# One kernel, one change: the RWKV-7 recurrence of a two-block transformer, from loops over pairs of heads to steps that work on three pairs at once, with 32-column inverses

## The chip, the cores and the metric

The kernel runs on one core of one Trainium2 chip. The metric is the time of one execution on the device in microseconds, as the median of several runs. PE is TensorE, DVE is VectorE, ACT is ScalarE, POOL is GpSimd, SP is SyncE.

## The reference, cut to what matters

The program is a whole network: two blocks with attention, gated linear attention and feed-forward parts over 512 tokens. The change touches one part of the second block, the recurrence of RWKV-7, with 8 heads of 64 features:

```
def rwkv7_scan(r, w, k, v, a_vec, b_vec):
    # per head, state S (N_v x N_k):
    # S_t = S_{t-1} diag(w_t) + (S_{t-1} a_t) b_t^T + v_t k_t^T ;  y_t = S_t r_t
    def step(state, inp):
        rt, wt, kt, vt, at, bt = inp
        sa = jnp.einsum('bhvk,bhk->bhv', state, at)
        state = state * wt[:, :, None, :] + sa[..., None] * bt[:, :, None, :] + vt[..., None] * kt[:, :, None, :]
        return state, jnp.einsum('bhvk,bhk->bhv', state, rt)
...
    kk = heads(k * rw_k_k, RW_N)
    kk = kk * lax.rsqrt(jnp.maximum(jnp.sum(kk * kk, -1, keepdims=True), 1e-24))
    k = k * (1 + (a - 1) * rw_k_a)
    y = rwkv7_scan(r_h, heads(decay, RW_N), k_h, v_h, -kk, kk * a_h)
...
    bonus = jnp.sum(r_h * k_h * rw_r_k, -1, keepdims=True) * v_h
```

The kernels compute it by chunks of 32 tokens. Inside of a chunk the recurrence is solved with the inverse of a triangular 32x32 matrix I - M, as the product of (I + M)(I + M^2)(I + M^4)(I + M^8)(I + M^16); across chunks a state is carried.

## The kernel before, in words

All is float32. Features lie on the 128 partitions (a pair of heads, 64 each), the 512 tokens along the free axis, as four tiles of 128 tokens, each of four chunks. `recurrence` (L3247) runs three stages one after another: `rwkv_prepare_stage` (decay, rate and gate), `rwkv_chunks_stage` (L2300 to L2733), which the change rewrites, and `rwkv_states_stage` (L2736), which carries the state over 16 chunks. No weights are loaded in this part.

`rwkv_chunks_stage` goes over four pairs of heads: a loop of three iterations on every engine and the last one as straight code (`over_pairs`, L2371). Every engine has its own order of work, and semaphores count its results. For a pair it does this:

- Operands, made one pair ahead by DVE, ACT and POOL between their other work: kk0, t, kx, scan, cx (`decays`, L2557), Ew, En, Ex (`exponentials`, L2671), the norm of the keys as a sum over a head by PE (`norm_sums`, L2453, one matmul of 512 columns), `reciprocal` of the whole 128x512 on DVE (L2577) and a square root on ACT (L2680), then kk, ah, bb, bh, kh, rk, rh and the bonus.
- PE (`pair`, L2460): TA, TB, TK and TV turn operands to tokens on partitions; BA, M and KA are products over the 64 features of each head, on the two halves of PE's rows (`fill_both`, L2423); DVE masks them to the chunk (L2620, L2627). A fill is what is written to one of seven PSUM banks, which are used in turn: a fill waits until the one seven places before has been taken by DVE or ACT (`free`, L2412).
- The inverse: M2, T2 (the square of M and of its transpose T), then for the powers 2, 4 and 8 a new M, a new T and X (the product so far), then X16. Each is a fill by `over_tiles` (L2434): four matmuls 128x128 by 128 columns, one per tile of tokens, of matrices that are zero outside of the four 32x32 blocks on the diagonal. ACT copies the new M and T (L2691), DVE adds X (L2636).
- P applies the inverse, Q are the queries, G the transitions and F the additions of the state of each chunk, Y the outputs inside of a chunk. For the sums over one chunk out of a tile's four, POOL writes copies of tok_b and tok_k with zeros in the other chunks' rows (Bm, Km, L2388), so that PE sums over all 128 rows: G as four matmuls of 256 columns per head (L2513), F as 64 matmuls of 64 columns (L2524, L2526).

POOL also multiplies the queries and G by decays (L2399, L2404) and copies v. At the start of the whole program POOL makes masks in a chain of single steps (`make_masks`, L139), ahead of the bias tables of the first attention (L1699 to L1717) and a DMA of the forget gates (L1678).

## Time and profile before

| | us |
|---|---|
| median of 3 runs | 2397.62 (2396.93 to 2399.07) |
| the profiled execution, its own time | 2404.41 |
| its span, first to last instruction | 2402.7 |
| busy in the span: PE, weight loads of PE (PEld), DVE, ACT, POOL | 2297.6, 1882.6, 1037.7, 870.6, 259.1 |
| PE instructions (records of matmuls) | 13903 |
| `rwkv_chunks_stage` in the span | 1036.0 to 1225.2 |
| mean granted clock of TensorE | 0.979 |

A busy PE is not PE at its peak, since matmuls overlap: a record's duration holds its passage through the array too. A float32 matmul leaves two records, and with each of them a weight load. What the engines do at one place is read from windows and timelines of that stretch, not from the shares of the span. The two slices of the page (60 us each) in which the DMA engines move almost nothing are those of this stage.

### The profile page before, as it was taken

What the parts mean: (1) busy time and instruction counts of PE and PEld (TensorE: products, weight loads), DVE (VectorE), ACT (ScalarE), POOL (GpSimd) and SP (SyncE); (2) the same over time, 40 slices, a digit from 0 to 9 for tenths busy, and PEclk for the clock granted to TensorE, in tenths of its full rate; (3) what the DMA queues carried; (4) which work ended last, traced back from release to release, by engine and by line L of the source; (5) the groups of instructions that cost most, each with busy time, mean ns of one, the idle gap of its engine ahead of it and who ended that gap; (6) DMA issues with size and microseconds to landing.
All of it is one profiled execution on the core that took longest, in us unless ns stands there. A gap on an engine that the chain in (4) does not pass through costs nothing. (4 is left out here: it accounts for less than half of the span.)

```text
span 2402.7 us, 33906 instructions
## 1 busy us (share of the span) xinstructions
PE 2297.6 (96%) x13903; PEld 1882.6 (78%) x13903; DVE 1037.7 (43%) x1593; ACT 870.6 (36%) x1511; POOL 259.1 (11%) x335
## 2 busy tenths in 40 slices
PE   8999999999999999879989999999999989999997
PEld 7777677988887877658868888888877779888886
DVE  4343335544334454356655443333533255333333
ACT  5444452423223352243413322222455544222223
POOL 4000000100000102023402200001422104000001
PEclk9999999999999999979999999999999999999998
DMA  5322123233333232100004233333242022333320
GB/s 163 84 53 61 46 80 88 77 99 96 95 92 93 63 105 71 37 0 1 0 2 114 74 99 96 97 92 93 71 86 60 19 77 73 94 99 98 96 87 36
DMA packets 346474, 178.38 MB, mean 74 GB/s; under 512 B 43927, under 2 KB 340037, under 8 KB 346333
## 3 DMA queue, kind: packets, MB, share of 16 engines
q1 hardware_dynamic: 344300, 171.54, 25.4%
q0 software_dynamic: 2032, 4.85, 0.7%
q8 instruction: 103, 1.69, 0.3%
q14 instruction: 39, 0.31, 0.0%
HBM read 171.35 MB, written 2.11 MB: 72 GB/s over the span
## 5 line engine op out<-in xcount | busy, mean ns | idle before, releaser
L428 DVE TENSOR_TENSOR w_lo<-w,w_hi 128x1024 fp32r<-128x1024 f32 (+2 forms) x327 | 398.1, 1220 | 437.9 <-ACT w_hi L421 437.5
L445 PE MATMUL bank<-act_hi,w_hi 128*128 128x512 f32 (+1 forms) x1496 | 564.9, 378 | 19.0 <-DVE act_lo L780 7.9
L447 PE MATMUL bank<-act_hi,w_lo 128*128 128x512 f32 (+1 forms) x1496 | 551.4, 369 | 0.0
L446 PE MATMUL bank<-act_lo,w_hi 128*128 128x512 f32 (+1 forms) x1496 | 550.1, 368 | 0.0
L421 ACT ACTIVATE w_hi<-w 128x1024 fp32r<-128x1024 f32 (+2 forms) x328 | 336.3, 1028 | 379.7 <-PE bank L447 255.9
L445 PEld LDWEIGHTS bank<-act_hi,w_hi 128*128 128x128 f32 x1496 | 284.0, 190 | 76.7 <-issue 15.0
L447 PEld LDWEIGHTS bank<-act_hi,w_lo 128*128 128x128 f32 x1496 | 283.9, 190 | 50.3
L446 PEld LDWEIGHTS bank<-act_lo,w_hi 128*128 128x128 f32 x1496 | 284.8, 190 | 46.2
L445 PE MATMUL bank<-hid_hi,w_hi 128*128 128x512 f32 (+1 forms) x560 | 207.7, 371 | 0.0
L447 PE MATMUL bank<-hid_hi,w_lo 128*128 128x512 f32 (+1 forms) x560 | 207.0, 370 | 0.0
L446 PE MATMUL bank<-hid_lo,w_hi 128*128 128x512 f32 (+1 forms) x560 | 206.4, 369 | 0.0
L445 PE MATMUL acc<-act_hi,w_hi 128*128 128x512 f32 (+1 forms) x480 | 175.6, 366 | 7.1 <-DVE act_lo L780 4.1
L446 PE MATMUL acc<-act_lo,w_hi 128*128 128x512 f32 (+1 forms) x480 | 174.3, 363 | 0.0
L447 PE MATMUL acc<-act_hi,w_lo 128*128 128x512 f32 (+1 forms) x480 | 174.2, 363 | 0.0
L663 DVE SCALAR_TENSOR_TENSOR x<-x,bank 128x512 f32<-128x512 f32 (+1 forms) x88 | 51.7, 588 | 192.5 <-PE bank L447 192.5
L445 PEld LDWEIGHTS bank<-hid_hi,w_hi 128*128 128x128 f32 x560 | 105.1, 188 | 21.0 <-issue 0.8
L446 PEld LDWEIGHTS bank<-hid_lo,w_hi 128*128 128x128 f32 x560 | 105.2, 188 | 20.2
L447 PEld LDWEIGHTS bank<-hid_hi,w_lo 128*128 128x128 f32 x560 | 105.3, 188 | 19.4
L445 PEld LDWEIGHTS acc<-act_hi,w_hi 128*128 128x128 f32 x480 | 91.7, 191 | 21.8 <-DVE w_lo L428 4.3
L447 PEld LDWEIGHTS acc<-act_hi,w_lo 128*128 128x128 f32 x480 | 91.6, 191 | 14.0
L446 PEld LDWEIGHTS acc<-act_lo,w_hi 128*128 128x128 f32 x480 | 91.7, 191 | 13.8
L714 ACT ACTIVATE hid_hi<-tmp_y 128x512 fp32r<-128x512 f32 (+1 forms) x48 | 28.6, 596 | 197.4 <-DVE tmp_y L724 197.4
(451 smaller groups left out, 3118.6 us busy)
## 6 DMA issues: line engine op xcount, KB each, us to landing
w<-in_ffn_w_gate_up SPq DMA_DIRECT2D x88, 512.0 KB, 3.8
w<-in_w_in SPq DMA_DIRECT2D x41, 512.0 KB, 3.9
w<-in_w_up SPq DMA_DIRECT2D x32, 512.0 KB, 4.0
w<-in_w_down SPq DMA_DIRECT2D x32, 512.0 KB, 3.9
w<-in_ffn_w_down SPq DMA_DIRECT2D x32, 512.0 KB, 4.0
w<-in_even_w_in SPq DMA_DIRECT2D x28, 512.0 KB, 3.8
w<-in_ffn_w_down SPq DMA_DIRECT2D x16, 384.0 KB, 3.4
w<-in_w_out SPq DMA_DIRECT2D x8, 512.0 KB, 3.9
```

The lines of the kernel that those rows point to most:

```text
L421: e.activation(self.split_of(part)[0][:, 0:part.n], w.raw[part.g % w.LOADS][:, 0:part.n], ACT.Copy)\
L428: e.tensor_tensor(w_lo[:, 0:part.n], w.raw[part.g % w.LOADS][:, 0:part.n], w_hi[:, 0:part.n].bitcast(F32), ALU.subtract).then_inc(w.lo.sem, 1)
L445: e.matmul(s.acc, *first, start=(k == 0), stop=False)
L446: e.matmul(s.acc, *second, start=False, stop=False)
L447: last = e.matmul(s.acc, *third, start=False, stop=(k == kt - 1))
L663: e.scalar_tensor_tensor(out=x, in0=x, scalar=self.alpha, in1=s.acc, op0=ALU.mult, op1=ALU.add)\
L714: e.activation(self.high(i)[:, s.cols], self.y[:, i % 2, s.cols], ACT.Copy).then_inc(g.act.sem, 1)
```

## The change

The stage has six steps instead of four iterations, all as straight code. Step n, from -2 to 3, does three things on every engine, cut into pieces that take turns: the sums of pair n (`pair(0)`, the tail: TA to TV, BA, KA, AV, P, Q, G, F, Y), the inverse of pair n + 1 (`pair(1)`, the chain: MT, the levels, X16) and the operands of pair n + 2 (`pair(2)`, ahead: norm, roots, bonus). So the first step has only operands, the last only sums. The name lists below give the order of the pieces on each engine.

The inverse is computed on the 32x32 blocks alone: M, T and X of all four chunks of a tile lie as [128, 4, 32] on partitions, and `over_chunks` multiplies each chunk's block on its own quarter of PE's rows and columns. `chunk_products` makes M and its transpose (MT) by blocks. T copies go from ACT to DVE. G and F are summed on quarters of the rows (`sums_of_chunks`), each chunk of a tile in its own bank, so the masked copies of POOL are gone; G and F are stored with the chunk before the tile, and the states stage (`of_chunk`) reads them so. The norm is summed into [128, 128] with the tokens' tiles on quarters of the partitions, the reciprocal and root are taken there, and ROOT, four matmuls, spreads it again. cx and kh are computed by POOL instead of DVE; bh, kh and ar have two buffers. v is read in place. `make_masks` adds up three 32-column masks in nine more links. Three increments of semaphores in the start (`COUNT_FROM`) are dropped.

The diff, cut to its core (removed lines of the stage are left out where the new ones stand for them):

```diff
@@ -170,6 +165,11 @@
         chain.link(e.tensor_copy(tri, core.in_chunk[:, :, 0:C32]))
         chain.link(e.affine_select(out=core.tri[:, n, :], in_=core.tri[:, n, :], compare_op=ALU.is_ge,
                                    fill=0.0, base=base, pattern=[[step, P]], channel_multiplier=-step))
+    for n, src in enumerate((core.tri[:, 0, :], core.tri[:, 2, :], core.ident[:, :])):
+        own, chunks = core.of_own_chunk[:, n, :], src.rearrange("p (c f) -> p c f", f=C32)
+        chain.link(e.tensor_tensor(own, chunks[:, 0, :], chunks[:, 1, :], ALU.add))
+        for c in range(2, CPT):
+            chain.link(e.tensor_tensor(own, own, chunks[:, c, :], ALU.add))
...
+    def in_order(*pieces):
+        return [f"{name}.{n + ahead}" for n in range(-2, PAIRS4) for ahead, names in pieces if 0 <= n + ahead < PAIRS4
+                for name in names]
+    pe_names = in_order((1, ["MT0", "MT1"]), (0, ["TA", "TB"] + both("BA") + both("KAa")), (1, both("M2", "T2")),
+                        (0, both("KAb") + ["TK", "TV"]), (1, both("M4", "TX4")), (2, ["NORM"]), (0, both("AV")),
+                        (1, both("M8", "TX8")), (0, both("P")), (1, both("M16", "X8")), (0, ["Q"]), (2, ["ROOT"]),
+                        (0, each("G")), (1, both("X16")), (0, each("F")), (2, ["BONUS"]), (0, ["Y"]))
+    dve_names = in_order((1, both("M", "T") + both("X1")), (0, both("BA") + both("KAa")), (1, both("T2")), (0, both("KAb")),
+                         (2, ["kk0", "t"]), (1, both("T4", "X2")), (2, ["kx", "scan"]), (1, both("T8", "X4")),
+                         (2, ["last", "NORM", "inverse"]), (1, both("X8")), (0, ["Q"]), (2, ["kk", "ah", "bb", "bh"]),
+                         (0, each("G")), (1, both("X16")), (2, ["rk", "rh", "BONUS"]))
+    act_names = in_order((0, ["TA", "TB"]), (1, both("M2")), (0, ["TK", "TV"]), (2, ["sq"]), (1, both("M4")), (0, both("AV")),
+                         (2, ["Ew", "En", "Ex"]), (1, both("M8")), (0, both("P")), (1, both("M16")), (2, ["root"]),
+                         (0, each("F") + ["Y"]))
+    pool_names = in_order((2, ["cx", "kh"]), (0, ["q_decayed", "G_decayed"]))
+    fills = [name for name in pe_names if name.split(".")[0] not in ("NORM", "ROOT", "BONUS")]
+    number = {name: n for n, name in enumerate(fills)}
...
+        TXs = [[[core.sb(c, f"rw_TX{n}{j}{s}", [P, NT, 2, C32]) for s in range(2)] for j in J] for n in range(2)]
         PP = av
-        bm = [core.sb(c, f"rw_bm{j}", [P, NT, CPT, HD]) for j in J]
-        km = [core.sb(c, f"rw_km{j}", [P, NT, CPT, HD]) for j in J]
...
+        def of_chunks(parts, p, ch):
+            return parts[ch // 2][:, p, ch % 2 * NT * HD:(ch % 2 + 1) * NT * HD]
...
+            def decays(p):
+                e.wait_ge(*dve.of(f"scan.{p}"))
+                pool.mark(e.tensor_tensor(cx[:, :], cw[:, :], decay[:, p, :], ALU.subtract), f"cx.{p}")
+            def keys(p):
+                e.wait_ge(*dve.of(f"kx.{p}"))
+                e.wait_ge(*act.of(f"En.{p}"))
+                if p >= 2:
+                    e.wait_ge(*pe.of(f"TV.{p - 2}"))
+                pool.mark(e.tensor_tensor(kh[p % 2][:, :], k2, En[:, :], ALU.mult), f"kh.{p}")
...
+            def over_chunks(lhsT, rhs, width):
                 def emit(b):
                     for t in range(NT):
+                        for ch in range(CPT):
+                            rows = slice(C32 * ch, C32 * ch + C32)
+                            last = e.matmul(b[rows, t * width:(t + 1) * width], lhsT[rows, t, :], rhs[rows, t],
+                                            start=True, stop=True)
                     return last
                 return emit
+            def sums_of_chunks(s, p, *products):
+                for ch in range(CPT):
+                    free(f"{s}{ch}.{p}")
+                for t in range(NT):
+                    for n, (lhsT, rhs) in enumerate(products):
+                        for ch in range(CPT):
+                            rows, b = slice(C32 * ch, C32 * ch + C32), bank_of(f"{s}{ch}.{p}")
+                            for j in J:
+                                last = e.matmul(b[HD * j:HD * j + HD, t * HD:(t + 1) * HD], lhsT(rows, t, j), rhs(rows, t, j),
+                                                start=(n == 0), stop=(n == len(products) - 1))
+                            if t == NT - 1 and n == len(products) - 1:
+                                pe.mark(last, f"{s}{ch}.{p}")
...
+            def norm_sums(p):
+                if p:
+                    e.wait_ge(*dve.of(f"BONUS.{p - 1}"))
+                e.wait_ge(*act.of(f"sq.{p}"))
+                for t in range(NT):
+                    last = e.matmul(ready_bank[32 * t:32 * t + 32, 0:P], core.head_ones[:, 3 * HD // 4:5 * HD // 4],
+                                    t_sq[:, t * P:(t + 1) * P], start=True, stop=True)
+                pe.mark(last, f"NORM.{p}")
+            def norm_roots(p):
+                e.wait_ge(*act.of(f"root.{p}"))
+                for t in range(NT):
+                    last = e.matmul(ready_bank[:, t * P:(t + 1) * P], core.pick_pair_head[:, t, :], norm[:, 2, :],
+                                    start=True, stop=True)
+                pe.mark(last, f"ROOT.{p}")
+            def bonus_sums(p):
+                e.wait_ge(*dve.of(f"rk.{p}"))
...
+            def chunk_products(p):
+                e.wait_ge(*dve.of(f"bh.{p}"))
+                for j in J:
+                    free(f"MT{j}.{p}")
+                a, b = ar[p % 2][:, 0, :], bh[p % 2]
+                for t in range(NT):
+                    for n, (left, right) in enumerate(((a, b), (b, a))):
+                        for ch in range(CPT):
+                            cols = slice(t * P + C32 * ch, t * P + C32 * ch + C32)
+                            for j in J:
+                                rows, out = slice(HD * j, HD * j + HD), bank_of(f"MT{j}.{p}")[C32 * ch:C32 * ch + C32, :]
+                                last = e.matmul(out[:, n * P + t * C32:n * P + (t + 1) * C32], left[rows, cols],
+                                                right[rows, cols], start=True, stop=True)
+                                if t == NT - 1 and n == 1 and ch == CPT - 1:
+                                    pe.mark(last, f"MT{j}.{p}")
...
+            def level(p, power):
+                for j in J:
+                    now, TX = Ms[j][power.bit_length() % 2 ^ 1], TXs[p % 2][j]
+                    if power == 1:
+                        fill(f"M2{j}.{p}", over_chunks(TX[0][:, :, 0, :], now, C32), dve.of(f"T{j}.{p}"))
+                        fill(f"T2{j}.{p}", over_chunks(now, TX[0][:, :, 0, :], C32))
                         continue
+                    both = TX[power.bit_length() % 2 ^ 1]
+                    fill(f"M{2 * power}{j}.{p}", over_chunks(both[:, :, 0, :], now, C32), dve.of(f"T{power}{j}.{p}"),
+                         act.of(f"M{power}{j}.{p}"))
+                    if power < 8:
+                        fill(f"TX{2 * power}{j}.{p}", over_chunks(now, both, 2 * C32), dve.of(f"X{power // 2}{j}.{p}"))
+                    else:
+                        fill(f"X8{j}.{p}", over_chunks(now, both[:, :, 1, :], C32), dve.of(f"X4{j}.{p}"))
...
+            def solve(p):
                 for j in J:
...
+            def transitions(p):
+                sums_of_chunks("G", p, (lambda rows, t, j: PP[j][rows, t, 0:HD], head(tok_b)))
+            def additions(p):
+                sums_of_chunks("F", p, (head(tok_b), lambda rows, t, j: PP[j][rows, t, HD:P]), (head(tok_k), head(tok_v)))
...
+            def key_norm(p):
+                e.wait_ge(*act.of(f"Ew.{p}"))
+                dve.mark(e.tensor_copy(last_w[:, p, :], Ew[:, C32 - 1:T:C32]), f"last.{p}")
+                e.wait_ge(*pe.of(f"NORM.{p}"))
+                dve.mark(ts(norm[:, 0, :], ready_bank[:, 0:P], 1e-24, None, ALU.max), f"NORM.{p}")
+                e.wait_ge(*dve.of(f"NORM.{p}"))
+                dve.mark(e.reciprocal(norm[:, 1, :], norm[:, 0, :]), f"inverse.{p}")
+            def keys(p):
+                e.wait_ge(*pe.of(f"ROOT.{p}"))
+                dve.mark(tt(kk, kk, ready_bank[:, :], ALU.mult), f"kk.{p}")
+                e.wait_ge(*act.of(f"Ex.{p}"))
+                e.wait_ge(*dve.of(f"kk.{p}"))
+                if p >= 2:
+                    e.wait_ge(*pe.of(f"KAb1.{p - 2}"))
+                dve.mark(stt(out=ar[p % 2][:, 0, :], in0=kk, scalar=-1.0, in1=cx[:, :], op0=ALU.mult, op1=ALU.mult), f"ah.{p}")
+                dve.mark(tt(kk, kk, rate[:, p, :], ALU.mult), f"bb.{p}")
+                e.wait_ge(*act.of(f"En.{p}"))
+                e.wait_ge(*dve.of(f"bb.{p}"))
+                dve.mark(tt(bh[p % 2][:, :], kk, En[:, :], ALU.mult), f"bh.{p}")
...
+            def squares(p):
+                for j in J:
+                    e.wait_ge(*pe.of(f"T2{j}.{p}"))
+                    dve.mark(e.tensor_copy(TXs[p % 2][j][1][:, :, 0, :], own(f"T2{j}.{p}")[:, :, 0, :]), f"T2{j}.{p}")
...
+            def last_levels(p, power):
+                for j in J:
+                    name, TX = f"X{power}{j}.{p}", TXs[p % 2][j]
+                    e.wait_ge(*pe.of(name))
+                    add(p, j, power, TX[power // 8 % 2], TX[power // 8 % 2 ^ 1], own(name)[:, :, 0, :])
```

## Rows read from the trace of the kernel before

**Rows 1.** Windows: stretch, length, busy (count) of PE, PEld, DVE, ACT, POOL, clock, DMA.
```profile
1036.00:1051.30 15.30, 3.92 (x4) 1.23 (x5) 12.42 (x16) 5.81 (x8) 0.61 (x1) 0.56 0.00 0
...
1051.30:1059.40 8.10, 8.10 (x65) 7.12 (x63) 4.06 (x7) 2.45 (x5) 5.45 (x8) 0.78 0.00 1
...
1059.40:1087.00 27.60, 25.64 (x212) 24.05 (x210) 22.19 (x30) 14.68 (x25) 8.31 (x10) 1.00 0.00 1
...
1096.60:1140.60 44.00, 41.26 (x470) 37.51 (x470) 29.98 (x40) 18.95 (x33) 17.43 (x20) 1.00 0.00 0
```

**Rows 2.** PE's timeline, second pair: start, us, engine, line, out<-in, shape, count, [wait].
```profile
1096.60 0.61 PE L2445 MATMUL rw_bank<-ident,rw_ar 128*128 128x128 f32 x4
...
1098.45 2.00 PE L2430 MATMUL rw_bank<-rw_ar,rw_bh 64*128 64x256 f32 x16
...
1100.28 1.06 PE L2430 MATMUL rw_bank<-rw_bh,rw_ar 64*128 64x128 f32 x16
...
1101.17 1.90 PE L2430 MATMUL rw_bank<-rw_ar,rw_kh 64*128 64x256 f32 x16
...
1105.14 1.10 PE L2438 MATMUL rw_bank<-rw_tok_v,rw_ka 128*128 128x64 f32 x8
...
1112.27 1.16 PE L2438 MATMUL rw_bank<-rw_XT,rw_M 128*128 128x128 f32 x8 [1.50 <-DVE rw_XT L2632]
...
1125.56 3.08 PE L2438 MATMUL rw_bank<-rw_XT,rw_M 128*128 128x128 f32 x24
...
1132.29 1.90 PE L2513 MATMUL rw_bank<-rw_bm,rw_av 128*64 128x256 f32 x16
...
1134.01 0.28 PE L2524 MATMUL rw_bank<-rw_av,rw_bm 128*64 128x64 f32 x4
...
1137.74 0.39 PE L2535 MATMUL rw_bank<-rw_ba,rw_av 128*64 128x128 f32 x4
...
1139.59 1.13 PE L2451 MATMUL rw_ready_bank<-rw_s,head_ones 128*128 128x512 f32 x2
...
1140.56 0.61 PE L2445 MATMUL rw_bank<-ident,rw_ar 128*128 128x128 f32 x4
```

**Rows 3.** PE's timeline, end of the preparation for the first pair.
```profile
1049.45 2.08 PE L2451 MATMUL rw_ready_bank<-rw_s,head_ones 128*128 128x512 f32 x2 [9.17 <-DVE rw_s L2595]
```

**Rows 4.** PE's timeline at three other places, with matmuls on parts of the array.
```profile
943.10 0.45 PE L2048 MATMUL bank<-gla_S,gla_grow 64*32 64x128 f32 x16
...
943.47 0.71 PE L2042 MATMUL bank<-gla_v,gla_AT 128*128 128x128 f32 x4
...
1225.16 0.45 PE L2770 MATMUL rws_step<-wide 64*64 64x64 f32 x8 [0.95 <-PEq L2334]
...
1993.62 1.10 PE L893 MATMUL norm_bank<-norm_squares,ones 128*32 128x64 f32 x64
```

**Rows 5.** Groups by form, 900 to 1260 us, DVE and ACT: busy, mean ns, idle before.
```profile
L2627 DVE TENSOR_TENSOR rw_ba<-rw_bank,tri 128x512 f32<-128x512 f32 x16 | 9.9, 683 | 9.6 <-PE rw_bank L2430 9.6
...
L2131 DVE TENSOR_TENSOR gla_AT<-bank,tri 128x256 f32<-128x256 f32 x8 | 3.0, 416 | 0.0
...
L2577 DVE RECIPROCAL rw_s<-rw_s 128x256 f32<-128x256 f32 x8 | 13.5, 1724 | 0.1
...
L2675 ACT ACT_TABLE_LOAD x4 | 5.1, 1283 | 0.1
```

**Rows 6.** POOL's timeline: the queries times their decays.
```profile
1133.61 1.29 POOL L2399 TENSOR_TENSOR rw_decay<-rw_decay,rw_last_w  x1 [20.93 <-DVE rw_decay L2645]
```

**Rows 7.** The page, DMA queues: packets, MB, share of 16 engines.
```profile
q8 instruction: 103, 1.69, 0.3%
```

**Rows 8.** POOL's timeline in the start: the DMA behind masks and bias tables.
```profile
44.10 0.55 POOL L1678 DMA_DIRECT2D fox_k<-f_cum  x1 [3.66 <-DVE f_cum L1662]
```

**Rows 9.** DVE's timeline: the first instruction of the stage.
```profile
1036.62 0.86 DVE L2561 TENSOR_SCALAR wide<-wide,vec 128x512 f32<-128x512 f32 x1 [1.87 <-PEq L2255]
```

More of the change, by code:

```diff
@@ L2329, in rwkv_chunks_stage @@
[L2329 to L2338 removed]
+    both = lambda *names: [f"{s}{j}" for j in J for s in names]
@@ L2419, in fill @@
+            def fill(name, emit, *needs):
+                free(name)
                 for need in needs:
@@ new lines, in values, with emit @@
+            def values(p):
+                e.wait_ge(*act.of(f"TV.{p}"))
+                for j in J:
+                    def emit(b):
+                        for t in range(NT):
+                            last = e.matmul(b[:, t * HD:(t + 1) * HD], ka[j][:, t, 0, :], tok_v[:, t, HD * j:HD * j + HD],
+                                            start=True, stop=True)
+                        return last
+                    fill(f"AV{j}.{p}", emit, dve.of(f"KAb{j}.{p}"))
+            def solve(p):
@@ L2664, in _ @@
+            over_steps(step)
         @block.scalar
         def _(e):
[L2666 to L2677 removed]
@@ new lines, in step @@
+            def step(pair):
+                tail, chain, ahead = pair(0), pair(1), pair(2)
+                if tail is not None:
+                    begin(tail)
+                if chain is not None:
+                    powers(chain, 2, 1)
+                if tail is not None:
+                    keys(tail)
+                if ahead is not None:
+                    squares(ahead)
+                if chain is not None:
+                    powers(chain, 4, 0)
+                if tail is not None:
+                    values(tail)
+                if ahead is not None:
+                    exponentials(ahead)
+                if chain is not None:
+                    powers(chain, 8, 1)
+                if tail is not None:
+                    solutions(tail)
+                if chain is not None:
+                    powers(chain, 16, 0)
+                if ahead is not None:
+                    root(ahead)
+                if tail is not None:
+                    finish(tail)
```

570 lines of the change are left out of this document (253 added, 317 removed).

## The prediction

> **What bounds the kernel now.** I read the page's slices first: PE is busy in all of them, and the only stretch in which the DMA engines are almost idle is the recurrence. Then the windows of that stretch [rows 1]: from 1036.0 to 1225.2 us the stage `rwkv_chunks_stage` runs 15.3 us of preparation and four pairs of heads, a pair in the loop taking 44.0 us with PE busy for 41.3 of them, DVE for 30.0, ACT for 19.0, POOL for 17.4. So PE bounds a pair, by its queue of matmuls. The timeline of PE through the second pair [rows 2] shows what they cost. A float32 matmul has two records (two passes). On the whole array 24 records of 128x128 with 128 moving columns last 3.08 us, with the 0.28 of the last in it: 0.11 us each, 0.89 for the eight of a fill over four tiles. On halves of the rows two records share that time: BA, 16 records with 256 columns, takes 1.83 us (1098.45 to 1100.28), M, 16 with 128, takes 0.89. PE's waits are short: 1.50 us for DVE's X1 is the longest; 44.0 less 41.3 busy leaves 2.7 in all. In the preparation [rows 1] the clock granted is 0.56, near the lower of its two levels, and PE is busy 3.9 of 15.3 us; there the chain of DVE, ACT and PE sets the time, with PE's BONUS sum at the end of it after 9.17 us of idle time [rows 3].
>
> **What the change does to PE, per pair.** The powers and the inverse of a 32-token chunk are computed on 32x32 blocks, four chunks at a time on the diagonal of the array, instead of as 128x128 matrices that hold zeros outside of the four blocks.
> - Removed: M and 22 fills of eight records (two M2, T2, M4, T4, X2, M8, T8, X4, M16, X8, X16, each over four tiles). At 0.89 us each that is 19.6, with M (16 records on halves) 0.89: 20.5 us.
> - Put in its place: 704 small records (MT 128, M2 with T2 128, M4 with TX4 128, M8 with TX8 128, M16 with X8 128, X16 64). Their price is not in the trace in just this form, so I bound it. A record on a quarter of the columns with 64 moving columns: 64 records last 1.10 us, less some 0.2 of the last, 0.014 us each; on eighths of the array with 128 moving columns 16 records need 0.37 until the next group [rows 4], though their last one's own 0.28 is in their 0.45, so that the sixteen start within 0.17, 11 ns apart with the step between the passes in it. I take 7 ns as the cheap end (a quarter of the 0.028 that 32 columns would take at 0.11 for 128) and 14 ns as the dear end of the good case; 10 ns for records with 32 moving columns, 14 for the 128 with 64 (TX4, TX8). MT 1.3, levels 1.3, 1.6, 1.6, 1.3, X16 0.65: 7.7 us. Gain 12.8 us of PE's time.
> - P keeps 128 moving columns: 64 records for 16, four side by side in the time of one: 16 times 0.11, 1.8 us, before and after.
> - BA loses the half of it that held T: 16 records with 256 columns (1.83 us) become 16 with 128 (0.89): gain 0.9.
> - G: 1.72 us (1132.29 to 1134.01 in [rows 2]) becomes 64 records at 10 ns, 0.65. F: 3.73 us (1134.01 to 1137.74) becomes 128 records, 1.3. Gain 3.5.
> - NORM, as dear as BONUS, becomes 0.25 (8 records on quarters); ROOT is new, eight full records, 0.9. The rest stays [rows 2]: TA to TV 1.85, KA 1.83, AV twice 0.9 (64 moving columns, but 1.10 as the others: the weights' columns bound it), Q 0.9, Y 1.85, BONUS 0.96.
> - More changes between shapes of tiles: some 17 a step. The group behind the 64x32 one starts 0.2 us after that one's last start (943.10 and 943.47 in [rows 4]), while 128 columns take 0.11: 0.1 more; 1.7 us, most of it new.
> A full step of three pairs then has 24 to 25 us of PE work for 41.
>
> **The other engines per step.** DVE: operations on 128x512 from PSUM last 0.68 and start 0.61 apart; 128x256 lasts 0.42, so 128x128 some 0.28, 0.21 apart [rows 5]. T copies and X sums (16 of them), two M, two T: 4.2 us for 10 before; the reciprocal on 128 columns 0.9 for 3.4; kh and cx go to POOL (1.2 off DVE). 18 to 19 us in all for 30. ACT: M copies at 128 columns, no T copies, F in four: 12 us for 19, with its two table loads of 1.28 [rows 5]. POOL: the 16 masked copies (13 to 15 us of its 17.4) go, cx and kh come at about 1.3 each, as q_decayed [rows 6]: 6 us. No engine but PE comes near its step. The loops become straight code: 1090 records a pair for 468, of which all four pairs are now fetched. The instruction queue took 0.3% of sixteen engines for 103 packets [rows 7], 1.1 us for 16 KB, and 16 KB is 128 records at 128 bytes: 34 packets for the stage in some 130 us, below a third of one engine's time. In a burst it is just as fast as 9 ns a record, one more reason for 10 and not 7. At the start POOL's masks grow by nine links of 0.36 us, 3.2 us; they are hidden by the 3.66 us that POOL waits for f_cum before fox_k [rows 8]; without that cover they would cost up to 3 us. The states stage reads the same slices in another place: nothing.
>
> **The path through a step.** I walked one full step in order with these durations (0 is MT's start). MT, TA, TB, BA, KAa to 4.2; level 1 to 5.6; KAb, TK, TV to 7.6; level 2 to 9.3; NORM, AV to 11.5; level 4 to 13.2; P to 15.1. Up to here PE hardly waits, since DVE and ACT serve one level while PE fills the other pair's banks. Then three waits stand where there were none. (a) ACT has Ew, En, Ex ahead of the M8 copies: they end at 15.3, level 8 runs 15.4 to 16.7: 0.3. (b) ROOT waits for ACT's root, which waits behind P, M16 and a table load, to 18.9, and G, X16 and F stand behind it on PE: 1.2 after Q at 17.7. (c) F's four banks are free only when DVE has added G0 to G2, and in DVE's queue kk, ah, bb and bh stand ahead of G: G2 ends at 23.8, so F starts at 23.9, 2.4 after X16. BONUS waits for rk, then Y ends at 28.1. Next MT follows. So 28.1 us a full step, of which there are two.
> The others: the first (operands of pair 0 only) takes 14.4, the 15.3 of before less 2.9 of reciprocal and NORM copy, plus 1.8 for ROOT at the low clock. The second (inverse of pair 0, operands of pair 1) is a serial chain with a cold clock: 24.1. The first full step begins cold: 2 more, as in 1051.3 to 1059.4 [rows 1], clock 0.78. The fifth (no operands ahead: wait b and most of c go) 22.3; the last (sums of pair 3 alone) 15.3.
> Sum: 14.4 + 24.1 + 28.1 + 2 + 28.1 + 22.3 + 15.3 = 134.3 us. PE's last record ends some 0.3 later. The same stretch is now 187.6: from DVE's first instruction at 1036.6 [rows 9] to the end of Y at 1224.2, 0.95 before the states stage's first matmul [rows 4]. That is 53 us less. Against the profiled execution (span 2402.7, time 2404.4) it gives a span of 2350; that execution lies 6.8 us above the median of the runs, so the median becomes 2397.6 - 53 = **2344.6 us**.
>
> **A rule against it.** In the states stage, 64x64 tiles on the diagonal write one bank, in different partitions: eight records with 64 moving columns last 0.45, less some 0.2 for the last one, 0.035 apart [rows 4], where passes one behind the other would take 0.055 each (half of the 0.11 for 128 columns). So they overlap. The Trainium skill (TensorEngine Tiling (Array Packing), Gotcha 1) says that different row tiles cannot access the same PSUM bank simultaneously. By that rule the four chunks of every M, T, X and P fill would go one after another; the row speaks against it, for two tiles.
>
> **Rivals.**
> 1. *The four row tiles of a bank take turns* (slower). Price: 448 records with 32 columns go from 10 to 29 ns (8.5 us), 128 with 64 from 14 to 56 (5.4), P's 64 from 28 to 110 (5.3): 19 us per pair. The waits take up 2 to 3 of it in a full step; 12 + 17 + 17 + 19 + 5 = 70 us over the stage. 2344.6 + 70 = 2415. It decides from the point at which these fills cost 13 us a pair more than I put them at. For it: nothing in the trace has four row tiles. Against: two overlap. Chance 0.07.
> 2. *The clock stays at the lower level through the stage*, since waits (b) and (c) and small tiles leave PE idle more often: PE's moving-bound work doubles (10.7 to 21.4 in the tail), a full step is 41; 14 + 24 + 41 + 41 + 36 + 27 = 183 for 187.6, so 2393, no change. Against: waits of 1.5 us left the clock at 1.00 [rows 1, 2]. Chance 0.04.
> 3. *Small records at 14 to 18 ns*, by fetching or issue: 770 records and 4 to 8 ns more, 3 to 6 us a step, four steps: 2357 to 2368. Chance 0.20.
> 4. *Small records at 7 ns and waits (b), (c) filled better*: 2334. Part of the forecast's range.
> That the change leaves the stage's order as it is can be ruled out: the operation lists differ on every engine.
>
> **The numbers.** Forecast 0.68 (its own range 2333 to 2354), rival 1 0.07, rival 2 0.04, rival 3 0.20, 0.01 left. The range 2331 to 2366 leaves out rivals 1 and 2, the dear end of rival 3 and some at the low end. A measurement tells about 0.2% (5 us). Faster: 0.68 + 0.20 + part of 2 = 0.90; same 0.03; slower 0.07.
>
> **What would show it.** In the profile after: 16391 PE records for 13903; a stage of 130 to 138 us; two equal steps of 27 to 29 us, with PE idle before ROOT (ACT) and before F (DVE, G); fills of M2 in about 0.3 us. Groups of 32 small records lasting over 0.9 us would be rival 1; a granted clock near 0.5 in the full steps rival 2. I am wrong if the full steps are below 24 or above 33 us.

## The result, and the profile after

The changed kernel takes 2374.85 us (median of 4 runs, 2370.71 to 2379.79) against 2397.27 (4 runs, 2396.33 to 2399.07): ratio 0.9898, 95% interval 0.9875 to 0.9922. That is 22.4 us less, where 53 were forecast, and above the forecast's range (2331 to 2366). Three of the ten runs of e2 below were slow ones, and its time leaves them out.

The page after, its head and queues:
```profile
span 2368.7 us, 38449 instructions
...
PE 2243.6 (95%) x16391; PEld 1830.6 (77%) x16391; DVE 1002.9 (42%) x1613; ACT 847.0 (36%) x1495; POOL 218.5 (9%) x292
...
q8 instruction: 130, 2.13, 0.4%
```
16391 records on PE, as counted ahead; 27 more packets on the instruction queue than in [rows 7], as counted too: 34 for the stage, less the 7 that it took before. The profiled execution (2370.71 us) is the fastest of the four. Its span is 34.0 us shorter than before, of which the stage gives 26.0: from DVE's first instruction at 1033.3 to the last record of Y at 1194.9 it takes 161.6 us, 187.6 before. The rest (3.3 ahead of the stage, 4.7 behind it) is hardly touched by the change; in the profiled executions of the changed kernel and of the runs below that are made from it, the stage begins between 1029.4 and 1041.2 us, and behind it they need between 1172.9 and 1179.9 us. So those few us are no gain, and the lengths of the stage say more about a change in it than a few us between two executions.

Windows of after, one for each of the six steps (stretch, length, busy and count of PE, PEld, DVE, ACT, POOL, clock, DMA), to be read against [rows 1]:
```profile
1033.30:1047.50 14.20, 4.49 (x18) 2.44 (x18) 8.49 (x13) 5.29 (x7) 2.51 (x2) 0.59 0.00 1
1047.50:1074.00 26.50, 15.77 (x727) 12.56 (x726) 13.15 (x34) 7.06 (x15) 2.53 (x2) 0.63 0.02 4
1074.00:1111.90 37.90, 30.16 (x1094) 25.52 (x1094) 20.23 (x46) 12.26 (x28) 6.22 (x7) 0.83 0.01 3
1111.90:1145.70 33.80, 29.18 (x1096) 24.95 (x1095) 20.27 (x45) 12.77 (x29) 6.23 (x7) 0.85 0.02 5
1145.70:1177.80 32.10, 26.50 (x1075) 23.44 (x1073) 10.47 (x31) 8.01 (x22) 3.20 (x5) 0.86 0.02 4
1177.80:1194.90 17.10, 14.87 (x369) 13.21 (x368) 5.79 (x11) 6.05 (x14) 3.20 (x5) 0.96 0.01 3
```
Forecast were 14.4, 24.1, 30.1, 28.1, 22.3 and 15.3 us. The first step is right, the second and the last are 2.4 and 1.8 too long; the three steps with a tail and a chain (the third to the fifth) are 7.8, 5.7 and 9.8 too long. The fifth says most: it has no key work ahead, DVE is busy for 10.5 of its 32.1 us and ACT for 8.0, and still it is only 1.7 us shorter than the one before it, which has 10 us more of DVE's work and nearly as many PE records (1096 for 1075).

What PE waited for in the two full steps of after, and in the fifth:
```profile
PE rw_bank L2438 <- issue: 6.5, 5, 2.4
PE rw_bank L2452 <- DVE rw_G_second L2740: 5.0, 2, 2.5
PE rw_ready_bank L2479 <- ACT rw_norm L2808: 0.7, 1, 0.7
...
PE rw_bank L2438 <- issue: 3.6, 3, 1.8
PE rw_bank L2452 <- issue: 1.6, 1, 1.6
PE rw_bank L2452 <- DVE rw_G_second L2740: 0.4, 1, 0.4
```
The waits of F for DVE's G adds and of ROOT for ACT are those of the forecast. New is "issue": PE waited for nothing that a semaphore shows. PE's timeline of the fifth step has these stops in the middle of fills:
```profile
1149.87 0.45 PE L2438 MATMUL rw_bank<-rw_M,rw_TX 32*32 32x32 f32 x32
1150.15 0.48 PE L2438 MATMUL rw_bank<-rw_TX,rw_M 32*32 32x32 f32 x32
...
1159.27 1.03 PE L2438 MATMUL rw_bank<-rw_av,rw_TX 32*32 32x128 f32 x26
1161.60 1.18 PE L2438 MATMUL rw_bank<-rw_av,rw_TX 32*32 32x128 f32 x35 [1.29 <-issue]
...
1163.31 0.39 PE L2438 MATMUL rw_bank<-rw_M,rw_TX 32*32 32x32 f32 x24
1165.54 0.33 PE L2438 MATMUL rw_bank<-rw_M,rw_TX 32*32 32x32 f32 x8 [1.85 <-issue]
```
Where nothing stops it, a fill of 32 small records takes 0.28 us (1149.87 to 1150.15), 9 ns a record, where 10 were forecast. But a fill stops after 24 of its 32 records for 1.85 us. Counted through the step, four such stops lie 126, 126 and 252 records apart. The DMA view of the fifth step (40 slices of 0.8 us) shows the packets:
```profile
GB/s 0 0 20 0 0 0 0 20 0 0 0 20 0 0 0 0 20 0 0 0 0 20 0 0 0 0 20 0 0 0 0 20 0 0 0 20 0 0 0 0
...
q8 instruction: 8, 0.13, 1.7%
```
Eight packets of 16 KB, each a page of code, at intervals of four or five slices (3.5 to 4.2 us, read in narrower windows), through the whole step; the shortest interval in the stage is 3.3 us. In narrower windows each stop has the same order: a packet that takes 0.9 to 1.4 us lands, 1.2 to 1.6 us later PE goes on, and 1.2 to 1.7 us after that the next packet starts (1163.10 to 1164.08, PE at 1165.54, the next at 1166.95). **Theory:** a page is 128 records (with their weight loads), and in straight code the next one comes 3.3 to 3.9 us after the last at the earliest, however fast PE goes through it. A full step's 1090 records are 8.5 pages, 28 to 33 us. (The expectations below say 1106, two records for each transposition; the trace shows one.) **Rivals:** the waits between the engines; the granted clock, which fell from 1.00 in the pairs of before to 0.83 to 0.86 in these steps, because of the small tiles; the records themselves.

### The profile page after: what moved, and what is told of

The parts are those of the page before. It is cut to its first block and busy times, and to the rows that moved or that the text cites. A ratio compares the mean times of both kernels' runs of the same rounds, so it can differ in the third digit from the quotient of the medians.

```text
span 2368.7 us, 38449 instructions
## 1 busy us (share of the span) xinstructions
PE 2243.6 (95%) x16391; PEld 1830.6 (77%) x16391; DVE 1002.9 (42%) x1613; ACT 847.0 (36%) x1495; POOL 218.5 (9%) x292
```

## The experiments

**Four kernels that change one thing each.** e1: DVE's G adds ahead of the key work.
```diff
-                if ahead is not None:
-                    keys(ahead)
                 if tail is not None:
                     keep_transitions(tail)
+                if ahead is not None:
+                    keys(ahead)
```


> VectorE's four G adds stand ahead of kk, ah, bb and bh; nothing else changes, TensorE's program is the same record for record. Theory (a fetched page of 128 TensorE records comes at most every 3.9 us, and a full step has 1106 records, 8.6 pages, 33.7 us): the two waits of F for VectorE's G adds (2.7 us each) go, but the pages come no sooner, so the median moves by 0 to -1.5 us against the changed kernel's 2374.9. Rival (the waits that I predicted, and bank waits, make the steps long): both waits are on the path, -5.4 us, to 2369.5. Rival (the granted clock): as the theory, 0 to -1.

e2: the chunk products on the whole array, with the identity as the stationary operand (the inverses are left out).
```diff
-                        for ch in range(CPT):
-                            rows = slice(C32 * ch, C32 * ch + C32)
-                            last = e.matmul(b[rows, t * width:(t + 1) * width], lhsT[rows, t, :], rhs[rows, t],
-                                            start=True, stop=True)
+                        last = e.matmul(b[:, t * width:(t + 1) * width], core.ident[:, :], rhs[:, t], start=True, stop=True)
```


> Every product of one 32x32 block with its own rows (levels, X16 and P) becomes four products of the whole array per fill, with the identity as the stationary operand: the products of the inverses are left out, every copy, add, wait and bank stays. 240 matmuls (480 records) fewer per full step, 626 records instead of 1106. Theory (fetching bounds): 4.9 pages are 19 us and bound nothing; the steps fall to what their work and waits take, about 27 us for the two full ones, 23 for the step without key work, 25 for the first chain; sum of the six steps 135 to 142 us instead of 161.6, median 2349 to 2356. Rival (waits between engines make the steps long): all of them stay, only TensorE's own time changes by less than 2 us per step, median 2369 to 2375. Rival (small tiles lower the granted clock, and that is the loss): the clock in the full steps rises to 1.0 and the median falls as in the theory; then the kernel with wide rows and small tiles must not gain.

e3: the same columns through the same small tiles with a quarter of the instructions (three of four blocks of the inverses are left out).
```diff
-                    for t in range(NT):
-                        for ch in range(CPT):
-                            rows = slice(C32 * ch, C32 * ch + C32)
-                            last = e.matmul(b[rows, t * width:(t + 1) * width], lhsT[rows, t, :], rhs[rows, t],
-                                            start=True, stop=True)
+                    for ch in range(CPT):
+                        rows = slice(C32 * ch, C32 * ch + C32)
+                        last = e.matmul(b[rows, 0:NT * width], lhsT[rows, 0, :], rhs[rows], start=True, stop=True)
```


> The same products of 32x32 tiles, but one matmul per chunk row over all four time tiles (its first tile's block as the stationary operand for all four) instead of four: the same columns through the same small tiles, a quarter of the records (626 instead of 1106 in a full step); three of four blocks of the inverses are left out. Theory (fetching bounds): as with the whole array, median 2349 to 2356, no idle time called issue inside the fills, one page fetched per 5 us or more. Rival (small tiles lower the clock): tiles are as small as before, so the clock stays at 0.85 and the median at 2368 to 2375. Rival (waits between engines): 2371 to 2375.

e4: 64 small products more in each step with a chain.
```diff
+                free(f"X161.{p}")
+                for n in range(64):
+                    rows = slice(C32 * (n % CPT), C32 * (n % CPT) + C32)
+                    e.matmul(bank_of(f"X161.{p}")[rows, 0:C32], core.ident[rows, 0:C32], core.ident[rows, 0:C32],
+                             start=True, stop=True)
```


> 64 products of 32x32 tiles of constants (128 records, one page) are added ahead of X16, in each of the four steps with a chain; nobody reads them. In two of the steps TensorE waits 2.7 us for VectorE right behind X16, so their 1.2 us of work would be hidden there. Theory (fetching bounds): one page more per step, 3.9 us in each of the three steps with a tail and 0 to 2 in the first, +12 us (10 to 14), median 2387. Rival (waits, or TensorE's work): 0 in two steps and 1.2 us in two, +2.4 us (0 to 4), median 2377.

Measured: e1 2371.4 us, ratio to before 0.9895 (0.9867 to 0.9922), the same as the changed kernel's 0.9898. e3 2353.3, 0.9811 (0.9784 to 0.9839). e4 2383.3, 0.9947 (0.9924 to 0.997). e2 2404.2, 1.0008 (0.998 to 1.0037). The kernel before was run again beside each group of experiments, and its median moved between 2397 and 2406 us; so between two groups the ratios compare better than the medians.

e3 did what fetching said. Its windows from the second step on:
```profile
1052.00:1074.40 22.40, 13.42 (x299) 9.19 (x302) 12.96 (x34) 6.94 (x15) 2.53 (x2) 0.73 0.01 1
1074.40:1103.00 28.60, 24.29 (x614) 18.26 (x613) 20.13 (x46) 11.91 (x28) 6.22 (x7) 0.96 0.01 3
1103.00:1135.50 32.50, 26.03 (x612) 19.12 (x610) 19.43 (x45) 12.61 (x29) 6.22 (x7) 0.89 0.01 3
1135.50:1158.60 23.10, 21.19 (x594) 16.33 (x592) 10.47 (x31) 7.89 (x22) 3.20 (x5) 1.00 0.01 3
1158.60:1175.50 16.90, 14.28 (x322) 11.39 (x320) 5.78 (x11) 5.98 (x14) 3.20 (x5) 1.00 0.01 3
```
The stage takes 137.6 us, 24.0 less than after (21.5 by the medians), with every wait between engines still there (F for G 5.3 us in the two full steps, 5.0 in after). The fifth step needs 23.1, forecast 22.3. And from the third step on the clock is at 0.89 to 1.00 with tiles as small as in after: small tiles are not what lowers it. The rivals of the waits and of small tiles fall; that the records themselves cost it is left to e11. Not all of the 24.0 are stops. PE's idle time called issue went from 15.7 us in the stage to 3.8, but other waits came in its place, and all its idle time fell by 6.8 only; the other 17.2 are busy time of PE, 121.0 for 103.8. Multiplied by the clock of each step, which is an estimate, 5 of them are work (e3's fills of 32 columns are cheaper too, 0.22 us for 0.28) and 12 go with the lower clock.

e1 shows why a wait taken away brings nothing here. PE's waits in its two full steps:
```profile
PE rw_bank L2438 <- issue: 6.9, 5, 2.4
PE rw_ready_bank L2485 <- DVE rw_sq L2675: 3.1, 2, 1.6
PE rw_bank L2452 <- issue: 2.1, 2, 1.1
PE rw_bank L2452 <- DVE rw_G_second L2740: 1.0, 2, 0.5
```
F's 5.0 us for G are down to 1.0. In their place stand 2.1 of issue at F itself, and 3.1 of BONUS for rk, which the G adds now keep waiting. The stage took 163.4 us, 1.8 more than in after.

e4 came out between by the medians, 8.5 us more than the changed kernel, and by the stage, 7.5 (169.1 us), where a page of 3.9 in three steps would be 12 and its work 2.4; by the ratios it is 11.8 us. The first two of the three steps got 1.2 and 4.8 us longer, and F's wait for G is gone from them: in its place PE's issue time rose from 6.5 to 14.2 us. So there the page was partly hidden by that wait. The third got 1.9 longer, where no wait hides a page; that stays open.

e2 fell outside of what every theory gave. Its records on the whole array cost far more than I put them at; PE's timeline in its second full step:
```profile
1137.99 1.06 PE L2436 MATMUL rw_bank<-rw_TX,ident 128*128 128x32 f32 x8
1138.88 1.06 PE L2436 MATMUL rw_bank<-rw_M,ident 128*128 128x32 f32 x8
```
0.9 us for eight, 0.11 each with 32 moving columns, what 128 cost in [rows 2]. With 128 stationary columns a record took that much with 32 moving ones too. So e2 has no say on fetching; it says what the change gained: 32 records in 0.28 us in place of eight in 0.89.

**The same records, in straight code and in a loop.** e5 puts a burst of small products into the loop body of the kernel before, e11 puts 256 in straight code and then 256 in a loop ahead of pair 0. Each was executed once; what is compared lies inside of that execution.
```diff
+                free("TA", it)
+                e.transpose(bank_of("TA")[:, 0:P], ar[:, 0, 0:P], core.ident[:, :])
+                for n in range(192):
+                    rows = slice(C32 * (n % CPT), C32 * (n % CPT) + C32)
+                    e.matmul(bank_of("TA")[rows, 0:C32], core.ident[rows, 0:C32], core.ident[rows, 0:C32],
+                             start=True, stop=True)
```


> The kernel before, whose pairs 0, 1 and 2 are one loop body and whose pair 3 is the same body once more in straight code, gets 192 products of 32x32 tiles of constants (384 records, three pages) ahead of TA in that body; nobody reads them. Theory (fetching costs, not the records): where the body is executed again from what is already there (pairs 1 and 2) the burst takes about 9 ns a record, 3.5 us, with no page fetched in it; in pair 0 and in the straight pair 3 it stops after each 128 records and takes 8 to 11 us, with a page fetched each 3.4 to 3.9 us. Rival (small records cost TensorE that much themselves, or through the clock): the burst takes the same time, about 8 to 11 us, in all four pairs. If the body is too long to be kept, pages are fetched in every pair and the four are equal too, but with a fetch beside each stop.


```diff
             bonus_sums(0, 0)
...
+            small(256)
+            with e.Fori(0, 8):
+                small(32)
             over_pairs(e, pair)
```


> The kernel before, with TensorE given, once, ahead of pair 0, 256 products of 32x32 tiles of constants in straight code (512 records, four pages) and then the same 256 as a loop of 8 times 32. Nobody reads them. Theory (fetching): the straight ones stop after each 128 records and take 3.4 to 3.9 us a page, 11 to 15 us in all, each stop beside a page fetch; the loop's 512 records take about 9 ns each and what 8 branches cost, 5 to 8 us, with no fetch from its second pass on. Rival (small records cost TensorE that much, by issue, bank or clock): both take the same time per record.

e5 gave the third case: its 384 records took 8.9, 11.1, 10.6 and 8.2 us in the four pairs, each with pages fetched beside it, so a body of 853 records isn't kept, while that of before, 468 records, was (no page on that queue from 1094.7 to 1195.8). It tells nothing between theory and rival.

e11 decides. Its timeline:
```profile
1049.37 3.41 PE L2549 MATMUL rw_bank<-ident 32*32 32x32 f32 x236
...
1054.12 1.29 PE L2549 MATMUL rw_bank<-ident 32*32 32x32 f32 x128 [1.33 <-issue]
...
1058.12 1.93 PE L2549 MATMUL rw_bank<-ident 32*32 32x32 f32 x128 [2.72 <-issue]
...
1061.85 8.00 PE L2549 MATMUL rw_bank<-ident 32*32 32x32 f32 x532 [1.80 <-issue]
...
1070.22 0.65 PE L2445 MATMUL rw_bank<-ident,rw_ar 128*128 128x128 f32 x4 [0.37 <-issue]
```
And its DMA view from 1049 to 1071 us, slices of 0.55:
```profile
GB/s 0 0 0 0 30 0 0 0 0 0 0 30 0 0 0 0 0 0 30 0 0 0 0 0 0 30 0 0 0 0 0 0 0 0 0 0 0 0 0 0
...
q8 instruction: 4, 0.07, 1.5%
```
The straight 512 records take 12.7 us, with three stops, 128 records apart, and a page each 3.8 to 4.0 us. The same 512 as a loop (the last 512 of the 532) take 7.5 us, with a gap of 0.2 to 0.3 at each branch and no other stop, and behind the page at its start the queue is silent. One instruction, one operand, one bank: what differs is whether the code was there. It isn't the clock either: windows over the two halves give 6.85 us busy at 0.63 for the straight ones and 7.26 at 0.70 for the loop, and the three stops are 5.9 us, more than the whole difference of 5.2.

**Fewer records for the same result.** e6: VectorE transposes 32x32 blocks, so T and its powers no longer come from PE. e7: e6 with e1's order. e8: e7 with G and F for both heads in one product.
```diff
-                        fill(f"T2{j}.{p}", over_chunks(now, TX[0][:, :, 0, :], C32))
...
-                    dve.mark(e.tensor_copy(TXs[p % 2][j][1][:, :, 0, :], own(f"T2{j}.{p}")[:, :, 0, :]), f"T2{j}.{p}")
+                    dve.mark(e.transpose(TXs[p % 2][j][1][:, :, 0, :], Ms[j][1][:, :, :]), f"T2{j}.{p}")
```


> The transposed powers T, T2, T4 and T8 are no longer products of TensorE: VectorE transposes each 32x32 block of M, M2, M4 and M8 in place of copying the product; 64 matmuls (128 records, one page) fewer per step with a chain, 978 records in a full one, and VectorE executes as many instructions as before. Theory (fetching bounds the steps): 2.5 to 3.9 us less in each of three steps, 0 to 1 in the first chain (each level now waits for one engine more), -8 to -12 us against the changed kernel, median 2363 to 2367. Rival (waits between engines bound the steps): each level gets longer by a copy and a transposition, 0 to +6 us, median 2375 to 2381. Rival (TensorE's own work at small records of 9 ns): -1.2 us per step at most, -3 to -4, median 2371.

> The one before (transposed powers by VectorE) with VectorE's G adds ahead of the key work. Theory: with a page fewer per step more of F's wait for G is on the path, so moving G gives 0 to -3 us against it, median 2361 to 2366. Rival (the wait is worth its whole 2.7 us in two steps once fetching is eased): -5 us.


```diff
-                            for j in J:
-                                last = e.matmul(b[HD * j:HD * j + HD, t * HD:(t + 1) * HD], lhsT(rows, t, j), rhs(rows, t, j),
+                            last = e.matmul(b[:, t * P:(t + 1) * P], lhsT(rows, t), rhs(rows, t),
                                             start=(n == 0), stop=(n == len(products) - 1))
```


> On top of the one before, G and F multiply both heads at once: one product of 32 rows with 128 columns for two of 64, half of what it writes is not read; 48 matmuls (96 records) fewer per step with a tail, 882 records in a full one, four ScalarE and four VectorE instructions more per step. Theory (fetching): 0.75 page less in four steps, 1.5 to 2.9 us each where pages still bound, 0 to 1 in the last: -4 to -9 us, median 2353 to 2361. Rival (TensorE's own work bounds): twice the columns for the same sums, +0.5 to +1 us per step, median 2363 to 2370.

e6 2358.9 us, ratio 0.9833 (0.9806 to 0.986): 16 less than the changed kernel, more than the 8 to 12 expected; the stage takes 148.0. Not all of it came where it was expected: the second step gave 3.5 us (0 to 1 expected), the three long ones 5.7, 2.9 and 1.3 (2.5 to 3.9 each). e7 2363.0, 0.9848 (0.9832 to 0.9865): no gain from the order, its wait again at BONUS (2.8 us in the two full steps) and at issue. e8 2373.3, 0.9894 (0.9875 to 0.9913): slower, and by more than the rival gave; the 4 to 9 us less by the theory of fetching were wrong here. Three quarters of a page fewer didn't help, since the engines behind PE were now late:
```profile
1129.54 1.27 PE L2449 MATMUL rw_bank<-rw_tok_b,rw_av 32*128 32x128 f32 x32
...
1133.61 0.50 PE L2449 MATMUL rw_bank<-rw_av,rw_tok_b 32*128 32x128 f32 x8 [2.12 <-DVE rw_G_second L2740]
...
1138.37 1.12 PE L2482 MATMUL rw_ready_bank<-rw_sq,head_ones 128*128 128x512 f32 x2 [2.69 <-DVE rw_sq L2671]
```
G takes 1.2 us in 32 records (0.84 in 64), and its adds, now two for each of the four, hold up F by 2.1 and BONUS by 2.7.

e9 is e6 with the inverse carried transposed, so that square and update share the stationary operand, and turned once at the end (the diff is against e6). e10 is e9 with the G adds first and BONUS behind Y; e12 has only these two moves, on the changed kernel.
```diff
-                    fill(f"M{2 * power}{j}.{p}", over_chunks(both[:, :, 0, :], now, C32), dve.of(f"T{power}{j}.{p}"),
-                         act.of(f"M{power}{j}.{p}"))
-                    fill(f"X{power}{j}.{p}", over_chunks(now, both[:, :, 1, :], C32), dve.of(f"X{power // 2}{j}.{p}"))
+                    fill(f"M{2 * power}{j}.{p}", over_chunks(T_, MZ, 2 * C32), dve.of(f"T{power}{j}.{p}"),
+                         dve.of(f"X{power // 2}{j}.{p}"), act.of(f"M{power}{j}.{p}"))
```


> On top of the transposed powers: the inverse is carried transposed (Z), so that its update has the same stationary operand as the next square and both are one product of 64 columns; X comes from Z by one block transposition by VectorE at the end. 96 matmuls (192 records, 1.5 pages) fewer per step with a chain, 786 records in a full one; VectorE executes two instructions more per step. Theory (fetching bounds the steps): 6.1 pages are 23 us, below what work and waits take, so the steps come to those of the run with wide rows (28.6, 32.5 and 23.1 us, against 32.2, 31.0 and 30.7 with transposed powers only): -6 to -12 us against 2358.9, most of it in the step without key work, median 2347 to 2353. Rival (waits between engines): 0 to +4, median 2359 to 2363, since each level now waits for ScalarE and two operations of VectorE. Rival (TensorE's own work): 192 records of 9 ns, -1.7 us per step at most, 2353 to 2356.


```diff
-                if ahead is not None:
-                    bonus_sums(ahead)
                 if tail is not None:
                     outputs(tail)
+                if ahead is not None:
+                    bonus_sums(ahead)
```


> The one before, with VectorE's G adds ahead of the key work and TensorE's BONUS sums behind Y instead of ahead of it. When only the G adds were moved, F's wait for them (2.5 us) went and a wait of BONUS for rk (1.2 to 1.6 us) came; behind Y that one should be covered. Theory: with fetching eased the two waits of 2.5 us are on the path, -3 to -5 us against the one before. Rival (what is late next takes it: ROOT behind ScalarE, or the chunk products behind bh): within 1 us of it.

> The changed kernel with its 1106 records per full step, and only the two moves of the last version: VectorE's G adds ahead of the key work, TensorE's BONUS sums behind Y. No wait of F for G and none of BONUS for rk should be left. Theory (with this many records fetching binds, and a wait taken away is spent waiting for pages): 0 to -2.5 us against 2374.9, median 2372.5 to 2375, and more idle time called issue. Rival (the order gives the same 5 us as with fewer records): median 2369 to 2371.

e9 2355.7 us, 0.9796 (0.9771 to 0.9821). Its median lies in the range of the rival of TensorE's own work (2353 to 2356) and above that of fetching (2347 to 2353); by the ratios it is 8.9 us below e6, by the stage 7.4, 5.6 of them in the step without key work, which is what fetching said. e10 2350.3, 0.9782 (0.9752 to 0.9812). e12 2371.2, 0.9868 (0.9848 to 0.9887). Steps and waits of e10, the fastest of all:
```profile
1051.30:1075.00 23.70, 13.41 (x406) 10.24 (x405) 13.70 (x36) 7.06 (x15) 2.53 (x2) 0.57 0.01 2
1075.00:1103.80 28.80, 23.96 (x771) 20.25 (x770) 19.14 (x47) 12.83 (x29) 6.30 (x7) 0.92 0.01 3
1103.80:1132.40 28.60, 23.63 (x771) 20.03 (x770) 19.13 (x47) 12.73 (x29) 6.29 (x7) 0.94 0.02 4
1132.40:1158.30 25.90, 21.92 (x753) 19.46 (x752) 11.71 (x34) 7.58 (x21) 3.19 (x5) 0.87 0.02 4
```
```profile
PE rw_bank L2439 <- DVE rw_T L2698: 3.1, 2, 1.6
PE rw_bank L2453 <- issue: 2.3, 2, 1.2
PE rw_ready_bank L2480 <- ACT rw_norm L2808: 2.0, 2, 1.0
```
The two waits of 2.5 us (F for G) are down to 0.5 each and BONUS's are gone. Issue is 2.3 us in the two full steps, for 6.5 in after; but e9, which still had those waits, had none there. So even here part of a wait taken away came back as a stop. Laid side by side, with the time per page of 128 records over the three long steps:

| kernel | records in a full step | three long steps, us | us a page | stage, us |
|---|---|---|---|---|
| e4 | 1218 | 39.1, 38.6, 34.0 | 3.9 | 169.1 |
| after | 1090 | 37.9, 33.8, 32.1 | 4.1 | 161.6 |
| e1 | 1090 | 37.4, 36.8, 31.5 | 4.2 | 163.4 |
| e12 | 1090 | 34.1, 36.7, 33.2 | 4.1 | 161.5 |
| e6 | 962 | 32.2, 30.9, 30.8 | 4.2 | 148.0 |
| e7 | 962 | 34.9, 32.8, 30.0 | 4.4 | 151.5 |
| e8 | 866 | 37.3, 35.4, 30.5 | 5.1 | 157.1 |
| e9 | 770 | 30.6, 29.4, 25.2 | 4.8 | 140.6 |
| e10 | 770 | 28.8, 28.6, 25.9 | 4.7 | 138.0 |
| e3 | 610 | 28.6, 32.5, 23.1 | 5.9 | 137.6 |

Down to 962 records the time goes with the pages, at 3.9 to 4.4 us each; below, a page costs more than that, and work and waits set more of the steps, most of all in e8. What the two moves gave can't be told. By the stages it is 2.6 us in e10 over e9 and 0.1 in e12 over the changed kernel, which is the theory; by the medians 5.4 and 3.6, and by the ratios 3.4 and 7.2, which is not. The intervals overlap in both. That the order pays only once fetching is eased is not shown. e6, e7, e9 and e10 are faster than both kernels (their intervals lie below the changed kernel's 0.9875), e10 by 2.2% of before (1.9 to 2.5).

## Why the prediction was wrong

- **Where it failed.** The sentence on fetching: "34 packets for the stage in some 130 us, below a third of one engine's time. In a burst it is just as fast as 9 ns a record." It took the time that a packet is on its way (about 1.1 us) for the time between packets. 34 pages at 3.9 us are 133 us, as long as the whole forecast stage, and the first step takes none of them. The kernel before did not show that time: in its whole trace PE has no idle time called issue, so nowhere in it does PE outrun its pages. The nearest are three pages in its states stage, which is straight code, 14 and 13 slices of 0.275 us apart. Its DMA view from 1230 to 1241 us:
```profile
GB/s 60 0 0 0 0 0 0 0 0 0 0 0 0 0 60 0 0 0 0 0 0 0 0 0 0 0 0 60 0 0 0 0 0 0 0 0 0 0 0 0
```
But PE's timeline has no stop there: 16 records start every 0.465 us, 29 ns a record, so that 128 of them last 3.7 us by their own work. This row shows that pages can come every 3.7 us. No 128 records in a row took less than that anywhere in before; the forecast asked for a record in 9 ns, three times as fast, and took for granted that the pages would keep up.
- **Its size.** e3 has the same columns with 610 records for 1090 in a full step: 137.6 us for the stage, 3.3 above the forecast. So fetching, with the lower clock that came with it, is up to 24.0 of the 27.3 us by which the stage was longer than the forecast; e3's fills of 32 columns are 0.06 us cheaper, some 3 us over the stage by an estimate (14 of them in a pair). Terms that were a little small are the rest. By the medians the miss is 30.3 us, 3 more than the stage's; they lie in how the two profiled executions stand to their medians (before 7 above, after 4 below) and in the 8 us outside of the stage.
- **Rival 3** had small records at 14 to 18 ns "by fetching or issue". The cause was right, the form wrong: at the upper clock a record costs 9 ns, with a stop of up to 2.5 us at the end of a page, and the price is per page. (At the lower clock it costs 14: e11's 128 records in 1.8 us at 0.50, 1.2 at 1.00.) Its 2357 to 2368 was too cheap.
- **Prices of the small records**: right. MT's 128 start in 1.2 us (1.3 forecast), a level's fill in 0.28 (0.33). **P** at 1.7 us in the last step (1.8 forecast). **G and F** were too cheap: 0.84 us for G's 64 records (0.65), and 1.8 for F's 128 in the last step (2.0 from 1191.21 to 1193.21, 0.18 of it a stop), where 1.3 were forecast.
- **Rival 1**, and the rule behind it: 32 records of four row tiles, writing one bank, start in 0.28 us, 9 ns apart, and four of P's, with 128 columns each, start within 0.02 us and take 0.11 together, the time of one. The rule of the Trainium skill (TensorEngine Tiling (Array Packing), Gotcha 1) is not what this case's trace shows, for four row tiles on the diagonal either.
- **Wait (c)**: F waited 2.5 us for G's adds in both full steps (2.4 forecast), but the time was not to be had: e1. **Wait (b)**: 0.7 in one full step (1.2). **Wait (a)** can't be told from the stops.
- **Rival 2** in part. In the three long steps the clock was neither at the lower level throughout nor at the upper: 0.83 to 0.86. BONUS's two records took 2.08 us in a stretch at 0.56 [rows 1, 3] and 1.12 in e10 (at 1102.78) at 1.00. In e3 and e10, with tiles as small and fewer stops, these steps were granted 0.87 to 1.00. That the stops lower the clock fits these rows, but nothing changed the clock alone; what it costs by itself, within the 12 us above, stays open.
- **The parts that hold**: the first step (14.2, 14.4 forecast), ACT 12.3 to 12.8 in a full step (12), POOL 6.2 (6), and the count of records. DVE took 20.2 us where 18 to 19 were forecast.
- **The masks in the start** cost nothing that can be seen, but not by the cover that was named. POOL's bias tables ran 4.0 us later (from 38.55 for 34.60), beside two instructions of DVE ahead of f_cum, which lasted 3.56 and 2.64 us for 2.05 and 0.67; so f_cum itself was late, and fox_k was sent at 47.8 for 44.1. At its 1000th record PE was 0.2 us behind before (197.1 for 196.9).

## What to carry to other kernels

Before a change that replaces few long instructions by many short ones, count instructions in pages, and ask whether any straight code in the trace already goes through its pages that fast. A page's share of the DMA engines doesn't tell it: here a page was on its way for about 1 us, and the next one came 3.3 to 4.2 us after the last. An interval at which PE doesn't stop doesn't tell it either; the price is read where PE stops in the middle of a fill, beside a packet of the instruction queue. Here 128 float32 records were a page, and straight code of records shorter than 26 to 33 ns on average ran at the speed of its fetching. Unrolling is then a cost of its own: the loop of before fetched nothing after its first pass. When fetching binds, waits taken away can turn into stops (e1), and what helped was fewer instructions: letting products share a stationary operand, and letting an idle engine transpose.

## What the runs showed of the hardware that I had not expected

- Code in straight line reached PE at one page of 128 records (and their 128 weight loads) per 3.3 us at best, in every run; in this stage the page itself was on its way for 0.9 to 1.5 us. The queue itself can be faster: at the branches of e5's loop two pages came 1.0 and 0.9 us apart (1100.50 and 1101.51, 1159.75 and 1160.62). A loop body of 468 records was kept, one of 853 was fetched anew in every pass.
- A branch of PE's loop cost 0.2 to 0.3 us (e11).
- A record with 128 stationary columns took 0.11 us with 32 moving columns as with 128 (e2); one of 32 by 32 took 9 ns beside its neighbours (14 at the lower clock).
- VectorE turned 32x32 blocks as a plain instruction in place of a copy: e6 has as many DVE instructions in a full step as after (46), busy 19.7 us for 20.2; a turn of 128x128 took 0.29 to 0.31 us.
